# A fused two-block transformer kernel: the latent projections taken from the undivided input, and the input's norm made behind them

## The reference, cut to what matters

```python
x = _rms_norm(h, attn_norm[layer])            # x = h * g / sqrt(mean(h^2) + eps)
proj = x @ w_in[layer]                        # 17 column tiles of 128 in the kernel
cq = _rms_norm(proj[..., 0:256], mla_q_norm)  # tiles 0, 1
ckv = _rms_norm(proj[..., 256:512], mla_kv_norm)  # tiles 2, 3
q = cq @ mla_w_uq;  k, v = ckv @ mla_w_ukv
```

## Time and profile before

| | |
|---|---|
| timed runs | 1436.36, 1437.57, 1438.05 us; median 1437.57 |
| profiled execution, first to last instruction | 1436.4 us; no other time of that execution is given |
| mean granted clock of TensorE | 0.994 |
| start of column tile 0 on PE | 16.88 us |
| start of the `w_uq` products | 46.42 us |
| start of `values(0)` | 59.40 us |
| input latents' raw blocks 0 to 3 issued | 5.81 to 7.57 us |

### The profile page before, as it was taken

One profiled execution on the slowest core, in us unless ns is written; L12 is line 12 of the kernel. 1 busy time (PEld: TensorE's weight loads), 2 busy tenths in 40 slices (PEclk: granted clock), 3 DMA queues, 4 the chain that ended last, 5 costly groups with the idle time before them and its releaser, 6 DMA issues.

```text
span 1436.4 us, 28641 instructions
## 1 busy us (share of the span) xinstructions
PE 1401.5 (98%) x9938; PEld 1263.5 (88%) x9938; DVE 964.9 (67%) x1667; ACT 677.2 (47%) x1028; POOL 701.7 (49%) x348
## 2 busy tenths in 40 slices
PE   7999999999999999999999999999999989999997
PEld 6877698999999999988888888999989967899997
DVE  4524646889888888766666665544455844799987
ACT  4433644445455555543333333444465446555553
POOL 4313256778866666644444444444423435355441
PEclk9999999999999999999999999999999989999999
DMA  7421046667755555567777777555553513455552
GB/s 289 130 78 45 31 135 188 195 195 218 221 184 183 182 181 180 175 220 231 239 228 237 233 236 221 177 190 188 178 169 123 183 48 118 133 191 175 179 187 72
DMA packets 89994, 250.16 MB, mean 174 GB/s; under 512 B 10048, under 2 KB 35920, under 8 KB 89296
## 3 DMA queue, kind: packets, MB, share of 16 engines
q1 hardware_dynamic: 86112, 238.20, 52.5%
q10 hardware_dynamic: 3824, 11.17, 2.1%
HBM read 234.09 MB, written 15.24 MB: 174 GB/s over the span
## 4 chain that ended last, share of the span: by engine, by line
PE 91%; DVE 6%; ACT 2%; issue 1%; POOL 0%; DMA 0%; DVEq 0%; ACTq 0%
PE ps L1754 47%; PE ps L2162 25%; PE ps L2149 4%; PE ps L2132 3%; PE ps L2022 1%; PE ps L1980 1%; PE ps L1769 1%; PE ps L2000 1%; PE ps L1950 1%; DVE big L1138 1%; DVE x_op L1147 1%; PE ps L1840 1%; DVE w_lo L1116 1%; PE ps L2103 0%; PE ps L1871 0%
## 5 line engine op out<-in xcount | busy, mean ns | idle before, releaser
L529 POOL TENSOR_TENSOR w_lo<-raw,w_hi 128x1024 fp32r<-128x1024 f32 x259 | 643.0, 2484 | 618.5 <-ACT w_hi L644 614.2
L1754 PE MATMUL ps<-x_op,w_hi 128*128 128x256 f32 (+1 forms) x3968 | 740.8, 287 | 7.8 <-DVE x_op L1147 2.4
L1754 PEld LDWEIGHTS ps<-x_op,w_hi 128*128 128x128 f32 x3968 | 620.5, 192 | 22.9 <-issue 10.6
L1754 PE MATMUL ps<-x_op,w_lo 128*128 128x256 f32 (+1 forms) x1984 | 562.4, 283 | 0.0
L644 ACT ACTIVATE w_hi<-raw 128x1024 fp32r<-128x1024 f32 x400 | 420.4, 1054 | 263.6 <-PE ps L2162 206.7
L1754 PEld LDWEIGHTS ps<-x_op,w_lo 128*128 128x128 f32 x1984 | 380.0, 192 | 0.0
L2162 PE MATMUL ps<-w_hi,h_op 128*128 128x512 f32 x1008 | 280.7, 395 | 0.0
L1116 DVE TENSOR_TENSOR w_lo<-raw,w_hi 128x1024 fp32r<-128x1024 f32 x141 | 184.5, 1308 | 99.9 <-ACT w_hi L644 99.4
L2162 PEld LDWEIGHTS ps<-w_hi,h_op 128*128 128x128 f32 x1008 | 187.5, 188 | 43.3 <-issue 0.2
L2162 PE MATMUL ps<-w_lo,h_op 128*128 128x512 f32 x504 | 158.6, 395 | 0.0
L1472 DVE TENSOR_TENSOR work<-route_t,ps 128x1536 bf16<-128x1536 bf16 x64 | 112.2, 1754 | 8.7
(11 more groups left out here) (287 smaller groups left out, 1207.1 us busy)
## 6 DMA issues: line engine op xcount, KB each, us to landing
raw<-blocks SPq DMA_DIRECT2D x404, 512.0 KB, 3.6
early_store<-kv_mem SPq DMA_DIRECT2D x96, 128.0 KB, 1.7
work<-early_store SPq DMA_DIRECT2D x96, 128.0 KB, 3.7
big<-consts ACTq DMA_DIRECT2D x2, 1336.0 KB, 6.8
big<-h_t ACTq DMA_DIRECT2D x4, 272.0 KB, 3.9
big<-bias_lines ACTq DMA_DIRECT2D x8, 136.0 KB, 2.6
bias_lines<-route_t ACTq DMA_DIRECT2D x4, 264.0 KB, 2.2
res<-mem_t SPq DMA_DIRECT2D x1, 1024.0 KB, 10.5
```

The lines of the kernel that those rows point to most:

```text
L529: pool.tensor_tensor(w_lo[:, s, :], raw[:, s, :], w_hi[:, s, :].bitcast(F32), ALU.subtract).then_inc(sem("lo_pool"), 1)
L1754: mm = pe.matmul(ps[:, m_bank, 0:T], w, x, start=(k == 0 and j == 0), stop=(k == last and j == 2))
```

## The change

1. Column tiles 0 to 3 are projected from a new operand `in_op` (parts hi and lo of h g): ACT makes the hi part straight from `h_t` as it arrives, DVE the lo part. In `undivided_in` the sixteen products with `w_hi` come first, the eight with `w_lo` behind them. `in_op` lies in the memory of `q_full` and `k_full`, so POOL clears those only when tiles 0 to 3 are done.
2. The norm of the input is made behind this. Its squares are folded on DVE, so PE sums 2 tiles in place of 8. `x_op` is needed first by tile 4. PE's `latent_sum` gets a third matmul, with `eps_r2` = 2 eps r^2.
3. The keep-warm row goes from 20 to 34 matmuls and to the front.
4. Half of `h_t` and all constants are issued by SP between the raw blocks, in place of by ACT; `w_uq`, `w_ukv` and `mem_t` come behind raw blocks 4, 5 and 6.
5. The orders of ACT, DVE and PE are rewritten: the squares and the root of the memory tokens move behind `evacuate_in(5)` and behind the 8 bias transfers, and DVE's memory norm behind both latent norms. Block 0's rest goes from POOL to DVE.

```diff
 sync:
-            sp.wait_ge(sem("h_loaded2"), 16)
+            for c in range(2, 4): ... dma_start(h_t chunk c) -> h_loaded{c}
+            sp.wait_ge(sem("h_loaded0"), 16)
-            for j in range(RING):
-                load(At(j))
-            sp.dma_start(flat2(mem_t[:, :, :]), dram["mem_t"]).then_inc(sem("mem_loaded"), 16)
+            load(At(0))
+            sp.wait_ge(sem("h_loaded3"), 16)
+            load(At(1))
+            sp.dma_start(kept[:, :], dram["consts"][:, 0:N_CONSTS_KEPT]).then_inc(sem("kept_loaded"), 16)
+            sp.dma_start(rel_in, dram["rel_bias"]).then_inc(sem("rel_loaded"), 16)
+            load(At(2))
+            sp.dma_start(cst, dram["consts"][:, N_CONSTS_KEPT:]).then_inc(sem("cst_loaded"), 16)
+            load(At(3))
...
 gpsimd:
+            los(B_IN, B_IN + 5)
+            norm_lo(R_ATTN, NK)
+            pool.wait_ge(sem("block_used"), UNDIVIDED_IN)
             pool.memset(flat2(q_full), 0.0)
+            pool.memset(flat2(k_full), 0.0).then_inc(sem("heads_zero"), 1)
...
 scalar:
             for c in range(4):
                 act.wait_ge(sem(f"h_loaded{c}"), 16)
+                for k in range(2 * c, 2 * c + 2):
+                    act.activation(in_op[:, 0, k, :], h_t[:, k, :], ACT.Copy, scale=pcol("attn", k)).then_inc(sem("in_hi"), 1)
+                if c == 1:
+                    his(1)
+            his(2)
+            for c in range(4):
                 squares(flat2(h_t)[:, 2 * c * NK:2 * (c + 1) * NK], 2 * c, NK, 2)
...
+            evacuate_in(0)
+            evacuate_in(1)
+            his(B_IN + 5)
+            lat_squares(0)
+            root(R_ATTN, NK)
+            act.wait_ge(sem("rms_root"), R_ATTN + 1)
+            act.activation(eps_r2, rt, ACT.Square, scale=math.sqrt(2 * EPS)).then_inc(sem("eps_r2"), 1)
+            norm_hi(R_ATTN, NK, 0, range(0, 3))
+            evacuate_in(2)
+            norm_hi(R_ATTN, NK, 0, range(3, 6))
+            lat_root(0)
+            evacuate_in(3)
+            lat_squares(1)
+            norm_hi(R_ATTN, NK, 0, range(6, 8))
+            line_out(0)
+            line_out(1)
+            evacuate_in(4)
+            lat_root(1)
+            line_out(2)
+            line_out(3)
+            evacuate_in(5)
             act.wait_ge(sem("mem_loaded"), 16)
             squares(flat2(mem_t[:, :, :]), 0, NQ, KT)
...
                     act.dma_start(bias[:, h, t, :], src).then_inc(sem("bias_loaded"), 16)
+            act.wait_ge(sem("rms_sum"), R_MEM + 1)
+            act.activation(mem_rt, ps[:, 3, 0:NQ], ACT.Sqrt, scale=1.0 / D, bias=E_MODEL).then_inc(sem("rms_root"), 1)
             evacuate_in(7)
...
 vector:
+                for k in range(2 * c, 2 * c + 2):
+                    dve.wait_ge(sem("in_hi"), k + 1)
+                    dve.scalar_tensor_tensor(out=in_op[:, 1, k, :], in0=h_t[:, k, :], scalar=pcol("attn", k),
+                                             in1=in_op[:, 0, k, :].bitcast(F32), op0=ALU.mult, op1=ALU.subtract).then_inc(sem("in_lo"), 1)
+                if c == 2:
+                    los(1)
+            los(2)
+            dve.wait_ge(sem("rms_squares"), KT)
+            step(dve.tensor_tensor(sq[:, 0:4 * NK], sq[:, 0:4 * NK], sq[:, 4 * NK:8 * NK], ALU.add))
+            dve.tensor_tensor(sq[:, 0:2 * NK], sq[:, 0:2 * NK], sq[:, 2 * NK:4 * NK], ALU.add).then_inc(sem("squares_folded"), 1)
+            los(4)
             norm(R_ATTN, h_t, "attn", NK)
             dve.wait_ge(sem("rel_loaded"), 16)
             dve.tensor_copy(rel_rep, rel_in.unsqueeze(2).to_broadcast([BUCKETS, DH, P])).then_inc(sem("rel_ready"), 1)
...
 tensor:
-            norm(R_ATTN, NK)
-            keep_warm(20, 5)
+            keep_warm(34, 5)
...
+            undivided_in(0)
+            undivided_in(1)
+            pe.wait_ge(sem("squares_folded"), 1)
+            for k in range(2):
+                mm = pe.matmul(ps[:, 2, 0:NK], ones[:, :], sq[:, k * NK:(k + 1) * NK], start=(k == 0), stop=(k == 1))
+            mm.then_inc(sem("rms_sum"), 1)
+            undivided_in(2)
+            latent_sum(0)
+            undivided_in(3)
             pe.wait_ge(sem("rel_ready"), 1)
             pe.wait_ge(sem("cst_loaded"), 16)
             relative_line(0)
+            project_in(4)
             relative_line(1)
+            latent_sum(1)
             relative_line(2)
             relative_line(3)
             pe.wait_ge(sem("wu_loaded"), 32)
...
             project_in(5)
+            pe.wait_ge(sem("lat_root"), 2)
+            norm(R_MEM, NQ, bank=3)
             project_in(6)
+            pe.wait_ge(sem("rms_root"), R_MEM + 1)
             pe.wait_ge(sem("lat_ready"), 2)
             values(0)
```

More of the change, by code:

```diff
@@ L99 @@
 N_CONSTS_KEPT = 2 * 128
+Q_FULL = 21682
+UNDIVIDED_IN = 4
 def taken(n):
@@ L110, in lo_owner @@
         return None
+    if n == 0:
+        return "dve"
     if B_QUERY <= n < B_V + 2:
@@ L167, in build @@
         h_op = sb("h_op", [P, 2, 2, NQ], F32R)
+        with nc.sbuf_tensor("before_q_full", [P, Q_FULL], F32):
+            with nc.sbuf_tensor("in_op", [P, 2, KT, NK], F32R) as in_op:
+                pass
         big = sb("big", [P, NKEYS * NQ])
@@ L441, in _ @@
             sp.dma_start(par[:, :], dram["params"]).then_inc(sem("par_loaded"), 16)
-            sp.wait_ge(sem("h_loaded2"), 16)
+            for c in range(2, 4):
+                at = slice(2 * c * NK, 2 * (c + 1) * NK)
+                sp.dma_start(flat2(h_t)[:, at], dram["h_t"][:, at]).then_inc(sem(f"h_loaded{c}"), 16)
+            sp.wait_ge(sem("h_loaded0"), 16)
             def load(n):
@@ L667, in root, with norm_hi @@
                 act.activation(rt[:, 0:T], ps[:, bank, 0:T], ACT.Sqrt, scale=1.0 / D, bias=E_MODEL).then_inc(sem("rms_root"), 1)
-            def norm_hi(r, T, n):
+            def norm_hi(r, T, n, tiles=range(KT)):
                 if n:
                     act.wait_ge(sem("block_used"), n)
-                for k in range(KT):
+                for k in tiles:
                     act.wait_ge(sem("rms_xf"), normed(r) + k + 1)
@@ L1176, in _ @@
             ins.then_inc(sem("heads_set"), 1)
[L1177 to L1184, removed]
             def latent_norm(w):
                 src, dst, n, gain = ((proj[:, 0:2, N_META:NK], cqn, NQ, "qn"), (proj[:, 2:4, :], ckvn, NK, "kvn"))[w]
-                r = (rt, rb)[w][:, 0:n]
+                r = lat_r[w]
                 dve.wait_ge(sem("lat_root"), w + 1)
@@ L1200, in _ @@
             los(B_IN + 8)
+            dve.wait_ge(sem("rms_root"), R_MEM + 1)
+            step(dve.reciprocal(mem_rb, mem_rt))
+            for k in range(KT):
+                ins = dve.scalar_tensor_tensor(out=mem_t[:, k, :], in0=mem_t[:, k, :], scalar=pcol("mem", k), in1=mem_rb,
+                                               op0=ALU.mult, op1=ALU.mult)
+            ins.then_inc(sem("rms_xf"), KT)
             dve.wait_ge(sem("bank_free"), M_IN + 5)
@@ L1804, in _, with undivided_in @@
             pe.wait_ge(sem("ones_set"), 1)
-            norm(R_ATTN, NK)
-            keep_warm(20, 5)
+            keep_warm(34, 5)
             def project_in(j, tiles=range(KT)):
                 n, m = B_IN + j, M_IN + j
-                project(At(n), m % 2, NK, bank_free(m), operand(R_ATTN) if j == 0 else None, tiles)
+                project(At(n), m % 2, NK, bank_free(m), operand(R_ATTN) if j == UNDIVIDED_IN else None, tiles)
+            def undivided_in(j):
+                n, m = At(B_IN + j), M_IN + j
+                if j == 0:
+                    pe.wait_ge(sem("hi_done"), 1)
+                else:
+                    arrived(n)
+                if bank_free(m) is not None:
+                    pe.wait_ge(*bank_free(m))
+                out, s = ps[:, m % 2, 0:NK], n.mod(RING)
+                for k in range(KT):
+                    if j == 0:
+                        pe.wait_ge(sem("in_lo"), k + 1)
+                    for part in range(2):
+                        pe.matmul(out, w_hi[:, s, k * P:k * P + P], in_op[:, part, k, :], start=(k == 0 and part == 0), stop=False)
+                if j == 0:
+                    arrived(n)
+                for k in range(KT):
+                    mm = pe.matmul(out, w_lo[:, s, k * P:k * P + P], in_op[:, 0, k, :], start=False, stop=(k == KT - 1))
+                mm.then_inc(sem("block_used"), 1)
             def relative_line(h):
```

65 lines of the change are left out of this document (19 added, 46 removed).

## The result

The changed kernel takes 1453.88 us as the median of four runs (1452.82 to 1454.43), the kernel before 1437.67 beside it (1436.36 to 1438.05): a ratio of 1.0117, with a 95% interval from 1.0105 to 1.0129. Forecast were 1447.5 and a range up to 1452.5. The sign and the place of every wait came as forecast; the size did not, and the time lies above the range.

What follows compares the result with a forecast made beforehand. TensorE's own work was taken to bound the kernel from 25.00 us on. Waits gave +6.5 us without falls, two clock falls 3.4: +9.9 on 1437.6 made 1447.5 us, range 1441 to 1452.5.

Steps and rivals of the forecast that it cites:

- the falls of the clock: TensorE's clock may drop to its lower level after each of four long waits; two falls taken, 3.4 us.
- the two stores: Ahead of line 3 and the w_uq products, ACT's copies wait for line stores that land 2.2 us after issue.
- The entry: Start of the kernel: tile 0 begins at 10.8 us, 6 us earlier than before, and tile 1 ends at 17.0.
- The fold: DVE's second fold of the input's squares waits for POOL's rest until 17.5 and ends at 18.2 us.
- The norm: Input's norm: root done at 19.9 us, the copy behind rel_ready at 30.6, TensorE idle 3.5 us.
- rival 3: Transfers bound the entry: raw block 4 lands at 21, root and all behind shift by 2.8 us, 1450.3; chance 0.07.
- The first latent's division is done by 35: Ahead of the w_uq products: this division ends by 35 us, so the products do not wait for it.
- Squares and root: TensorE idles 2.5 us ahead of the memory sum for ACT's squares, 4.3 ahead of values(0) for the root.
- The gain of 10 us or so: What an unbroken row of tiles from 10.8 us would bring, said to be spent in five waits.
- where I expect none: Behind values(0): no difference was expected there, and one arising would show the forecast wrong.
- Rival 2: The clock falls after all four long waits: +13.3 us, 1450.9; chance 0.20.

Runs made afterwards that it cites:

- rel_only: Changed kernel with DVE's copy of the position bias moved from behind the input's norm to ahead of the fold of the squares: 1445.24 us.
- lines_early: As rel_only, with the four lines spread over the tiles and ACT's copies moved along: 1444.57 us.
- all_early: lines_early with the memory tokens' squares and root early, and raw loads from block 9 on behind the line stores: 1435.56 us.
- late_loads: Changed kernel with SP issuing raw block 9 and all behind it only when the four line stores have landed: 1450.37 us.
- fill_waits: Changed kernel with matmuls that nobody reads put into its five long waits, none of which is taken away: 1444.25 us.
- root_early: Changed kernel with ACT making the memory tokens' root ahead of evacuate_in(6) and the 8 bias transfers: 1447.73 us.
- all_early_warm: all_early with 12 matmuls that nobody reads put ahead of tile 4: 1435.63 us.
- before_later: Kernel before with 112 in place of 20 keep-warm matmuls ahead of tile 0: 1452.02 us.
- both_early: As root_early, with the memory tokens' squares also moved ahead of evacuate_in(5): 1444.28 us.

## Why the prediction was wrong in its size

The waits were where it had put them. Two terms of its sum failed: the falls of the clock, 3.4 us taken and 9.8 measured, and the two stores, 4.4 us taken and 7.8 measured.

- **The entry** was right: tile 0 started at 10.21 (forecast 10.8), with tile 1 ending at 16.9 (17.0).
- **The fold** was right, in mechanism and time. DVE's second add against POOL's rest, in the profile after:

```profile
15.81 2.77 DVE L1196 TENSOR_TENSOR big<-big 128x544 f32<-128x544 f32 x1
```

```profile
15.48 2.52 POOL L555 TENSOR_TENSOR w_lo<-raw,w_hi 128x1024 fp32r<-128x1024 f32 x1 [12.59 <-ACT w_hi L671]
```

  It ended at 18.6 (forecast 18.2). The Trainium skill's rule on the shared ports of VectorE and GpSimd ("SBUF — State Buffer", section "SBUF: two separate sides") fits again.
- **The norm** until `rel_ready`: 31.4, forecast 30.6, and this near hit is in part luck. The root was to be done at 19.9, "held by block 4's rounding no longer than this"; DVE's reciprocal behind it started at 21.28. Raw block 3, behind the constants on SP's queue, took 9.5 us and landed at 18.04. ACT stood 2.4 us for it, then had block 4's rounding and the latent squares ahead of the root. This is rival 3's mechanism in a small form, 1.4 us; the chain behind it was 0.6 us shorter than its forecast of 10.7. ACT's timeline after:

```profile
18.06 1.06 ACT L671 ACTIVATE w_hi<-raw 128x1024 fp32r<-128x1024 f32 x1 [2.38 <-DMA raw<-blocks]
```

  Tile 4's operand was there at the same time as `rel_ready`, but the forecast took line 0 and tile 4 as strictly serial, right for this order and, as `rel_only` showed, the very thing to change. "The first latent's division is done by 35" was wrong too: it ended just ahead of 39, behind the copies that took 4.15 us. The products, at 50.35, did not feel it; in `lines_early` and `all_early` it became their wait.
- **The stores** failed as a term: two at 2.2 us, measured 3.83 and 3.97. The row gives a median over four; the first of them had taken 5.4 beside loads, which I had read and left out. 3.4 us too little, and `late_loads` gave 3.5 back. The first of the changed kernel's four, with no load issued just ahead of it, took 2.0.
- **Squares and root** were right: waits of 2.7 and 4.5 us (forecast 2.5 and 4.3). On the rule of the Trainium skill that issuing is usually small beside the transfer ("DMA: Bandwidth & Descriptors", section "Issuing engines are not separate DMA queues"), the trace agrees for one issue (0.45 us beside a median of 3.0 to landing); what cost was the eight in a row, 3.9 us from the first one's start to the last one's end, with the root behind them on ACT. ACT's timeline after:

```profile
74.62 3.54 ACTq L813 DMA_DIRECT2D big<-bias_lines  x7
...
78.21 0.47 ACT L815 ACTIVATE big<-ps,eps 128x256 f32<-128x256 f32 x1 [3.21 <-issue]
```

- **The falls of the clock** were the step that failed most, "I take two, 3.4", with "all four 6.8" as the bound. Four came, behind five long waits (the two ahead of line 3 and of the products share one). Line 0 and tile 4 took 3.3 us longer, the products 2.8, the memory sum 1.7, `values` 2.0, together 9.8. The price of 1.7 was that of the one fall at the entry of before, which lasted 3.4 us. The last two here lasted 3.4 as well, but the first 6.8 and the second 10.2. Why a fall lasts longer stays open: the first had TensorE busy in all of it, and in `rel_only` one of 13.7 us had it idle for 1.7. `fill_waits` gave 9.1 us of the 9.8 back by itself, and the timed median fell by 9.6.
- **"The gain of 10 us or so"** of an unbroken row of tiles does not fit the sum it stands in: its five waits are 14.7 us, and 14.7 less 6.5 leaves a gain of 8.2. The forecast does not rest on it.

The ledger to the end of `values(1)`: forecast +6.5 without falls, 0.8 for the norm, 3.3 + 2.8 + 1.7 + 2.0 for the falls, 3.4 for the stores and 0.4 for the waits make 20.9, measured 84.13 - 62.83 = 21.3. Behind it, "where I expect none", 5.4 came back, and this the forecast had named as a sign of being wrong: 4.3 of it in the stretch without a fall, 1.1 in a shorter row of waits near 1054 us. So the miss of 6.4 us by the timed medians flatters the forecast: at the yardstick it was 21.3 against 9.9. Rival 2 (all four falls) was the nearest, and the range should have counted falls of more than 1.7 and slower stores.

## What to carry to other kernels

Starting a bound engine earlier gains nothing by itself. Read what each wait ahead of the next fixed piece stands for, and put behind a semaphore only what needs it. Here tile 0 started 6.7 us earlier and `key_spread` 21.3 us later, because of an early copy that stood behind a long chain (8.6 us by the medians), a root behind eight transfer issues (6.2), squares behind an evacuation, and loads ahead of a store on the path (3.5). In a better order the same idea is 5 us faster than before. When you forecast a wait of a few us on TensorE, add a term for the clock behind it, and give that term a wide range: here it was 9.8 us for five waits of 17 us in all. Removing such a wait took both away (`root_early`), filling it took only the clock's part, and a filling in the wrong place held up work (`all_early_warm`).

## What the runs showed of the hardware

- Two VectorE copies of 8 partitions, with one input each, took 0.88 and 0.89 us with GpSimd idle, 4.15 us while it cleared memory (3.7 us of writes alone, changed kernel), and 6.97 us where a subtraction of 2.7 us followed the clearing (`all_early`). The held ones ended 0.7 and 0.3 us behind GpSimd. The Trainium skill ("SBUF — State Buffer", section "Who interferes with whom") names copies among the instructions that can take the shared ports, and the trace agrees.
- Clock levels after a wait: behind one of 4.4 us TensorE worked 0.2 us at full pace, then the clock fell to 0.50 for 6.8 us although it was busy from there on; behind one of 2.7 us (the memory sum's) it fell for 3.4; behind one of 1.2 us, in `rel_only`, it fell 2.9 us after the wait's end and for 13.7.
- A 264 KB store took 2.0 to 2.4 us in `late_loads`, with no load issued ahead of it, and 3.8 to 4.0 behind one 512 KB load.
- One kernel's executions spread with the clock: 1447.83 us at a mean clock of 0.999, 1451.79 to 1453.48 at 0.995 (`before_later`), and 1437.94 to 1448.46 at 0.994 to 0.988 (`both_early`).
